# Two neighbourhood attentions of a two-block model: where the attention steps of the third and fourth head group stand among the weight products

## The chip, the core and the metric

The kernel runs on one core of a Trainium2 chip. Its engines are TensorE (PE), VectorE (DVE), ScalarE (ACT), GpSimd (POOL) and SyncE (SP); each works through its own instructions in order, and they meet through semaphores. The metric is the device time in microseconds of one execution, the median over several.

## The reference

Two blocks run one after the other on x of 256 tokens by 1024 features, in float32. The first has a dilated attention, an mLSTM and two SwiGLU feed-forwards. The second has four layers, each a mixer and an MLP with squared ReLU; the mixers are neighbourhood attention (layer 0), a conformer convolution (1), a short gated convolution (2) and neighbourhood attention again (3). Beside the 256 latent tokens the second block has 256 context tokens; they are carried along up to layer 2, so layer 0 computes attention for both, layer 3 for the latent tokens alone. This is the attention, cut:

```python
def neighbourhood_attention(h_lat, h_ctx, wqkv, wo, rpb, ctx_out):
    q, k, v = split_heads(h_lat @ wqkv, 3)          # 16 heads of 64
    q = q * ATTN_SCALE
    if ctx_out:
        q_c, k_c, v_c = split_heads(h_ctx @ wqkv, 3)
    else:
        k_c, v_c = split_heads(h_ctx @ wqkv[:, D_MODEL:], 2)
...
        s_lat = jnp.einsum("bhqd,bhaqkd->bhqak", q_r, k_nb)   # window of the latent grid
        s_lat = s_lat + bias_r                                 # a bias by relative position
        s_ctx = jnp.einsum("bhqd,bhcd->bhqc", q_r, k_c)
        p = jax.nn.softmax(jnp.concatenate([s_lat, s_ctx], axis=-1))
        return p_lat @ v_nb + p_ctx @ v_c
...
    o_lat = o_grid @ wo
    if ctx_out:                                     # context tokens attend to context only
        p_c = jax.nn.softmax((q_c * ATTN_SCALE) @ k_c.T)
        o_ctx = (p_c @ v_c) @ wo
    return o_lat, o_ctx
```

## The kernel before

Activations lie feature-major: 8 tiles of 128 features, each 256 latent and 256 context columns wide. Every weight is read once as a **unit** of up to 1024 rows by 256 columns (1 MB). SP loads it into one of three `raw` buffers; ACT rounds it to `hi` and DVE takes the rest, `lo = raw - hi` (a **split**, two halves of 128 x 1024 on each engine, L1359, L1360, L1656, L1659). A product is three fp32r matmuls (hi x hi, hi x lo, lo x hi; L1149 to L1151 feature-major, L1170 to L1172 for token-major values). There are two buffers of split halves and three raw ones, so the split of a unit waits until the unit two before it is used, and the load of a unit until the split of the unit three before it is done.

`plan()` writes the program as one list of steps; each engine goes through this list and issues its part of each step. So the order of the list is the order on every engine. The split of unit j + 1 is written just ahead of the products of unit j. `linear` and `linear_tok` write the products of a unit; between them they call `advance`, which takes the next step of the first entry of `background`. `adv` says how many steps are taken in one tile of a unit (8 contraction steps k), spread evenly by `share`; `outer=True` runs both tiles of a unit together, k by k. A bare `yield True` in a background generator is a step that writes nothing.

`neighbourhood` takes the 16 heads in four groups of four heads (`group`), two heads to a tile `q` of 128 features. For each group it writes three units: q, k and v. Behind them the group's attention `heads(group)` goes into `background`, and is so spread over the three units of the next group. The attention of a group has these steps:

- `lat_scores(q, qb)`, four in a group: the scores of one block `qb` of 128 latent queries for two heads, into two PSUM banks (PE, L1282); DVE adds the bias table and takes the maximum (L1938), negates it (L1947), ACT takes the exponentials (L1547), DVE the reciprocal (L1949) and scales (L1953). DVE's part stands in one piece in its order, so it holds DVE while ACT works. It also writes `table(i + 2)`.
- `ctx_scores(q)`, two in a group and in layer 0 only: the context queries (PE L1291; DVE L1961, L1964, L1968; ACT L1558).
- `turn(n, q, which)`: transposes of the probabilities through the identity (PE L1302), copied back by ACT (bank one, L1565) and DVE (bank two, L1973).
- `mix(q, ctx, ...)`: probabilities by values (PE L1314); ACT rounds the result to the high half of `OB` (L1570), DVE makes the low half (L1978).

The bias tables (`table(i)`, i from 0 to 15, one for each latent score step) are POOL's: four DMAs from `na_rpb` into `NB` (L2119), a wait for them, two additions of the mask (L2123). There are two table buffers, so table i + 2 waits until DVE has taken the maximum of score step i (L1947 reads it).

After the last group `grow` writes the four units of the output projection `na_wo_2`. Its first unit runs both tiles together; before its contraction step k the function from `stages_for` takes steps from the background until the tile k of the attention's output is made, and then `adv` 6 asks for more. Since `heads(3)` enters the background just ahead of it, all attention of the last group lies in this first unit. PSUM banks are handed out in turn, six of them, so the bank numbers change when steps change places. `credit` and `pace` decide at the end of tiles whether a row of the modulation matrix is computed on DVE (L1735), with its DMA on POOL.

## Time and profile before

| | us |
|---|---|
| median of 3 runs | 3013.59 |
| lowest, highest | 3011.38, 3013.71 |
| the profiled execution, its device time | 3015.04 |
| its span, first to last instruction | 3013.1 |
| PE busy in it | 2899.0 (96%) |
| DVE busy | 2000.8 (66%) |
| ACT busy | 1197.6 (40%) |
| POOL busy | 352.4 (12%) |

The span is cut by the place in the program. Layer 0's attention runs from about 869 to 1140 us, layer 3's from about 2600 to 2815. A matmul's duration in the trace contains its way through the array, so matmuls that follow each other overlap; what one costs PE is the distance between two starts. A wait is shown in brackets behind the row that ended it, with the instruction that it waited for. The granted clock (PEclk) is the share of TensorE's full 2.4 GHz, 0.5 being the lower level of 1.2 GHz. In the rows "NB" stands for the bias tables too, since they lie in the same memory, and "PB", "PT" for the probabilities and their transposes.

### The profile page before, as it was taken

To read this page: it belongs to the slowest core of one execution; us is meant where nothing else is said; L and a number is where in the kernel's file an instruction comes from. 1 tells how busy PE (TensorE), PEld (TensorE's weight loads), DVE (VectorE), ACT (ScalarE), POOL (GpSimd) and SP (SyncE) were. 2 spreads that over 40 slices of the span, in tenths; PEclk is the share of its full clock that TensorE was granted. 3 is DMA by queue.
4 is the path that set the end of the run, shared out by engine and by line. 5 is a ranking of instruction groups with operands and counts; after the bars stand their busy time and mean duration, and the time that the engine had idled before them with its cause. 6 is when DMAs were issued, how large, how long until landed. Compare 5 with 4: busy or idle time off the path is not lost.

```text
span 3013.1 us, 42743 instructions
## 1 busy us (share of the span) xinstructions
PE 2899.0 (96%) x17730; PEld 2511.1 (83%) x17730; DVE 2000.8 (66%) x3252; ACT 1197.6 (40%) x1953; POOL 352.4 (12%) x545
## 2 busy tenths in 40 slices
PE   7999999989999989999999999999999999998998
PEld 7999998879977768888864888888888888876998
DVE  6776777658745557777644776777777667654665
ACT  5444444644444434223312632223234222443543
POOL 0000000000113220000122100001010000243000
PEclk9999999989999999999999999999999999999999
DMA  6444675347755523544464254553535545565453
GB/s 216 154 154 140 212 239 190 127 140 246 238 113 84 83 56 123 171 155 159 129 188 119 84 161 161 161 168 122 166 125 168 161 154 169 125 107 82 136 186 127
DMA packets 362275, 451.88 MB, mean 150 GB/s; under 512 B 12656, under 2 KB 332432, under 8 KB 362080
## 3 DMA queue, kind: packets, MB, share of 16 engines
q1 hardware_dynamic: 326976, 329.89, 33.7%
q0 software_dynamic: 34944, 118.65, 16.5%
q8 instruction: 140, 2.29, 0.3%
q10 hardware_dynamic: 160, 0.59, 0.1%
q14 instruction: 55, 0.45, 0.0%
HBM read 438.67 MB, written 1.05 MB: 146 GB/s over the span
## 4 chain that ended last, share of the span: by engine, by line
PE 84%; DVE 9%; ACT 4%; DMA 1%; issue 1%; POOL 1%; DVEq 0%; ACTq 0%; POOLq 0%
PE ps L1149 24%; PE ps L1151 24%; PE ps L1150 24%; PE ps L1327 2%; PE ps L1170 2%; PE ps L1171 1%; PE ps L1172 1%; DVE lo L1656 1%; PE ps L1314 1%; DVE NB L1690 1%; DVE lo L1659 1%; ACT hi L1359 1%; PE ps L1302 1%; PE ps L1282 1%; PE ps L1182 1%
## 5 line engine op out<-in xcount | busy, mean ns | idle before, releaser
L1149 PE MATMUL ps<-XN,hi 128*128 128x256 f32 (+1 forms) x3120 | 1037.3, 332 | 46.0 <-DVE XN L1903 11.3
L1150 PE MATMUL ps<-XN,hi 128*128 128x256 f32 (+1 forms) x3120 | 1020.1, 327 | 0.0
L1151 PE MATMUL ps<-XN,lo 128*128 128x256 f32 (+1 forms) x3120 | 1019.6, 327 | 0.0
L1149 PEld LDWEIGHTS ps<-XN,hi 128*128 128x128 f32 x3120 | 598.7, 192 | 122.4 <-issue 14.5
L1151 PEld LDWEIGHTS ps<-XN,lo 128*128 128x128 f32 x3120 | 598.9, 192 | 49.0
L1150 PEld LDWEIGHTS ps<-XN,hi 128*128 128x128 f32 x3120 | 599.4, 192 | 47.6
L1735 DVE CUSTOM_DVE_ANT_0 MX<-MW,C 128x1024 bf16<-128x1024 f32 x384 | 480.0, 1250 | 109.3 <-DMA MW<-in_mod_w 102.5
L1656 DVE TENSOR_TENSOR lo<-raw,hi 128x1024 fp32r<-128x1024 f32 (+1 forms) x313 | 383.9, 1227 | 242.7 <-ACT hi L1359 241.6
L1359 ACT ACTIVATE hi<-raw 128x1024 fp32r<-128x1024 f32 (+1 forms) x313 | 326.2, 1042 | 428.6 <-PE ps L1151 428.4
L1659 DVE TENSOR_TENSOR lo<-raw,hi 128x1024 fp32r<-128x1024 f32 (+1 forms) x313 | 380.3, 1215 | 0.0
L1149 PE MATMUL ps<-H,hi 128*128 128x512 f32 (+1 forms) x1072 | 380.2, 355 | 0.0
L1150 PE MATMUL ps<-H,hi 128*128 128x512 f32 (+1 forms) x1072 | 379.7, 354 | 0.0
L1151 PE MATMUL ps<-H,lo 128*128 128x512 f32 (+1 forms) x1072 | 379.7, 354 | 0.0
L1360 ACT ACTIVATE hi<-raw 128x1024 fp32r<-128x1024 f32 (+1 forms) x313 | 324.6, 1037 | 0.0
L2078 POOL DMA_DIRECT2D MW<-in_mod_w x192 | 103.0, 537 | 1451.0 <-DVE mod L1735 1341.6
L1150 PEld LDWEIGHTS ps<-H,hi 128*128 128x128 f32 x1072 | 202.7, 189 | 28.4
L1149 PEld LDWEIGHTS ps<-H,hi 128*128 128x128 f32 x1072 | 202.7, 189 | 28.2
L1151 PEld LDWEIGHTS ps<-H,lo 128*128 128x128 f32 x1072 | 202.7, 189 | 28.0
L1727 DVE SCALAR_TENSOR_TENSOR X<-ps,mod,X 128x256 f32<-128x256 f32 x244 | 108.2, 479 | 139.1 <-PE ps L1151 139.1
L2084 POOL TENSOR_TENSOR SA<-SA,NB 128x256 f32<-128x256 f32 (+1 forms) x69 | 70.4, 1020 | 812.5 <-ACT NB L1367 811.7
L1170 PE MATMUL ps<-hi,XN 128*128 128x256 f32 x512 | 151.5, 296 | 0.1
L1171 PE MATMUL ps<-lo,XN 128*128 128x256 f32 x512 | 145.5, 284 | 0.0
(239 smaller groups left out, 3402.8 us busy)
## 6 DMA issues: line engine op xcount, KB each, us to landing
raw<-in_mlp_w SPq DMA_DIRECT2D x128, 1024.0 KB, 5.4
MW<-in_mod_w POOLq DMA_DIRECT2D x192, 512.0 KB, 3.8
raw<-in_ffn_w_in SPq DMA_DIRECT2D x44, 1024.0 KB, 5.1
raw<-in_attn_w_in SPq DMA_DIRECT2D x36, 1024.0 KB, 4.8
raw<-in_na_wqkv SPq DMA_DIRECT2D x24, 1024.0 KB, 5.4
raw<-in_ffn_w_out SPq DMA_DIRECT2D x16, 1024.0 KB, 5.3
raw<-in_mlstm_w_in SPq DMA_DIRECT2D x12, 1024.0 KB, 5.0
raw<-in_cv_w SPq DMA_DIRECT2D x12, 1024.0 KB, 6.2
```

The lines of the kernel that those rows point to most:

```text
L1149: e.matmul(out, whi, xhi, start=first, stop=False)
L1150: e.matmul(out, whi, xlo, start=False, stop=False)
L1151: i = e.matmul(out, wlo, xhi, start=False, stop=last)
L1170: e.matmul(out, xhi, hi[:, k, :], start=k == 0, stop=False)
L1171: e.matmul(out, xhi, lo[:, k, :], start=False, stop=False)
L1359: e.activation(hi[:, a:b], raw[:, a:b], ACT.Copy).then_inc(*high.says(("hi", j, 0)))
L1360: e.activation(hi[:, b:c], raw[:, b:c], ACT.Copy).then_inc(*high.says(("hi", j, 1)))
L1656: e.tensor_tensor(lo[:, a:b], raw[:, a:b], hi[:, a:b].bitcast(F32), ALU.subtract).then_inc(*low.says(("lo", j, 0)))
L1659: e.tensor_tensor(lo[:, b:c], raw[:, b:c], hi[:, b:c].bitcast(F32), ALU.subtract).then_inc(*low.says(("lo", j, 1), ("spent", j)))
L1727: e.scalar_tensor_tensor(out=m.X[:, j, a:b], in0=src[:, a:b], scalar=mod_of(m, gate, j, i), in1=m.X[:, j, a:b], op0=ALU.mult, op1=ALU.add) ...
L1735: e.tensor_tensor_reduce(out=m.MX[:, :], in0=m.MW[:, :], in1=m.C[:, s, :], scale=1.0, scalar=0.0, op0=ALU.mult, op1=ALU.add, accum_out=m.m ...
L2078: e.dma_start(m.MW[:, :], T["mod_w_2"][n // 48][n % 48 * P:(n % 48 + 1) * P, :]).then_inc(*sig["mw"].says(("mod_raw", n)))
```

## The change

All of it is in `neighbourhood`, so both layers 0 and 3 are touched.

- In `heads`: an empty step after the first two scores; the score step of the second query tile's second block comes ahead of the first tile's mix in layer 3 (it stood behind it); in layer 0 an empty step more ahead of that mix; ahead of every mix a loop yields until the group's values are made.
- In the loop over groups: for group 3 `heads(3)` enters the background behind the units of q and k, ahead of v. In group 3's units `adv` rises: q from 2 to 4 and k from 2 to 4 in layer 0, q from 1 to 2 and k from 2 to 3 in layer 3. The value unit has `adv` 3 in place of 2 in layer 0, for all groups, and in layer 3 for group 3. These units carry the third group's attention (`heads(2)`), group 3's value unit also the start of `heads(3)`.
- For groups 0 to 2 the background is drained before the next group's attention enters it. Two loops that did part of this are gone.

```diff
--- before.py
+++ after.py
@@ -803,6 +803,7 @@
         yield True
         s1 = lat_scores(0, 1)
         yield True
+        yield True
         for q in range(2):
             turn(s0, q, 0)
             yield True
@@ -815,12 +816,19 @@
             if q == 0:
                 s0 = lat_scores(1, 0)
                 yield True
+            if q == 0 and not ctx_out:
+                s1 = lat_scores(1, 1)
+                yield True
+            if ctx_out:
+                yield True
+            while ("v", layer, group) not in p.made:
+                yield True
             mix(q, False, *lat)
             yield True
             if ctx_out:
                 turn(sc, q, 2)
                 yield True
-            if q == 0:
+            if ctx_out and q == 0:
                 s1 = lat_scores(1, 1)
                 yield True
             if ctx_out:
@@ -829,8 +837,6 @@
 
     for group in range(4):
         def evac_q(t, b, u):
-            while len(p.background) > 1:
-                p.advance()
             p.do("na_q", layer, group, t, n, b, u)
 
         def evac_k(t, b, u):
@@ -840,15 +846,21 @@
             p.do("na_v", layer, group, t, b, u)
 
         streams = group == 0 and not ctx_out
-        p.linear("na_wqkv_2", slot, 0, KT, group * 256, 256, ("xn", s, 0, n), evac_q, adv=2 if ctx_out else 1,
-                 outer=group == 0, streams=(0,) if streams else None)
-        p.linear("na_wqkv_2", slot, 0, KT, 1024 + group * 256, 256, ("xn", s, 0, 512), evac_k, adv=2,
-                 outer=streams, streams=(0, 1) if streams else None)
-        p.linear_tok("na_wqkv_2", slot, 2048 + group * 256, 256, 4, ("xn", s, 0, 512), evac_v, adv=2)
+        p.linear("na_wqkv_2", slot, 0, KT, group * 256, 256, ("xn", s, 0, n), evac_q,
+                 adv=4 if ctx_out and group == 3 else 2 if ctx_out or group == 3 else 1, outer=group == 0,
+                 streams=(0,) if streams else None)
+        p.linear("na_wqkv_2", slot, 0, KT, 1024 + group * 256, 256, ("xn", s, 0, 512), evac_k,
+                 adv=4 if ctx_out and group == 3 else 3 if group == 3 else 2, outer=streams, streams=(0, 1) if streams else None)
         p.flush()
-        while len(p.background) > 1:
-            p.advance()
-        p.background.append(heads(group))
+        if group == 3:
+            p.background.append(heads(group))
+        p.linear_tok("na_wqkv_2", slot, 2048 + group * 256, 256, 4, ("xn", s, 0, 512), evac_v,
+                     adv=3 if ctx_out or group == 3 else 2)
+        p.made.add(("v", layer, group))
+        p.flush()
+        if group < 3:
+            p.drain()
+            p.background.append(heads(group))
     p.grow(("ob", layer, 0, n), n, (layer, 2), "na_wo_2", slot,
            p.stages_for(lambda k: ("ob", layer, k) in p.made), 6)
```

The order of the instructions shows it at two places. The first is PE in layer 0, around the first scores of the last group (`KB,QB` are scores, `OB` products of the output projection, `XN` with 256 columns products of the value unit; the digit after `ps` is the PSUM bank). Before:

```order
L1151 MATMUL ps3<-OB,lo1 128x512
L1282 MATMUL ps5<-KB,QB 128x512
L1282 MATMUL ps0<-KB,QB 128x512
L1149 MATMUL ps2<-OB,hi1 128x512
L1150 MATMUL ps2<-OB,hi1 128x512
L1151 MATMUL ps2<-OB,lo1 128x512
L1149 MATMUL ps3<-OB,hi1 128x512
L1150 MATMUL ps3<-OB,hi1 128x512
L1151 MATMUL ps3<-OB,lo1 128x512
L1282 MATMUL ps1<-KB,QB 128x512
L1282 MATMUL ps4<-KB,QB 128x512
```

With the change (its line numbers are 12 higher):

```order
L1184 MATMUL ps2<-hi0,XN 128x256
L1294 MATMUL ps3<-KB,QB 128x512
L1294 MATMUL ps4<-KB,QB 128x512
L1182 MATMUL ps2<-hi0,XN 128x256
L1183 MATMUL ps2<-lo0,XN 128x256
L1184 MATMUL ps2<-hi0,XN 128x256
L1182 MATMUL ps2<-hi0,XN 128x256
L1183 MATMUL ps2<-lo0,XN 128x256
L1184 MATMUL ps2<-hi0,XN 128x256
L1294 MATMUL ps5<-KB,QB 128x512
L1294 MATMUL ps0<-KB,QB 128x512
```

The last group's first two scores stood between products of `na_wo_2`; now they stand between products of the value unit, one unit earlier.

The second is DVE at the end of layer 3's attention, from the last latent softmax to the first residual (`lo<-raw,hi` is a weights' split, `OB` a mix's low half, `PT` a copy of a transpose, `X` the residual). Before:

```order
L1938 ISA stat 128x1
L1947 TENSOR_SCALAR stat<-stat 128x2
L1949 RECIPROCAL stat<-stat 128x2
L1953 TENSOR_SCALAR PB<-PB,stat 128x512 x2
L1973 COPY PT<-ps 128x4x128 x2
L1978 TENSOR_TENSOR OB<-ps,OB 128x256
L1727 SCALAR_TENSOR_TENSOR X<-ps,mod,X 128x256 x2
```

With the change:

```order
L1959 TENSOR_SCALAR stat<-stat 128x2
L1961 RECIPROCAL stat<-stat 128x2
L1965 TENSOR_SCALAR PB<-PB,stat 128x512 x2
L1668 TENSOR_TENSOR lo<-raw,hi 128x1024
L1671 TENSOR_TENSOR lo<-raw,hi 128x1024
L1990 TENSOR_TENSOR OB<-ps,OB 128x256
L1985 COPY PT<-ps 128x4x128 x2
L1990 TENSOR_TENSOR OB<-ps,OB 128x256
L1739 SCALAR_TENSOR_TENSOR X<-ps,mod,X 128x256 x2
```

A split now stands between the last softmax and the copies of the last transposes, and with it the low half of the other mix.

## Rows read from the trace of the kernel before

**Rows 1.** The page, busy time, share and count of PE and its loads.

```profile
PE 2899.0 (96%) x17730; PEld 2511.1 (83%) x17730; DVE 2000.8 (66%) x3252; ACT 1197.6 (40%) x1953; POOL 352.4 (12%) x545
```

**Rows 2.** Windows: stretch, its us, then PE, PEld, DVE, ACT, POOL, PEclk, DMA.

```profile
1000.20:1053.90 53.70, 52.74 (x321) 40.06 (x320) 28.84 (x64) 23.52 (x57) 16.13 (x25) 1.00 0.55 89
1053.90:1102.50 48.60, 37.21 (x187) 23.23 (x186) 25.19 (x62) 17.16 (x46) 7.83 (x12) 0.93 0.23 33
2761.10:2796.10 35.00, 23.89 (x130) 16.93 (x129) 15.92 (x41) 11.16 (x25) 8.51 (x14) 0.80 0.30 46
2704.80:2708.80 4.00, 3.99 (x20) 3.88 (x20) 1.24 (x2) 0.60 (x1) 0.00 (x0) 0.57 0.81 134
```

**Rows 3.** PE's timeline, layer 0, squeezed unit: start, us, instruction, [idle before <-releaser].

```profile
1083.51 0.57 PE L1149 MATMUL ps<-OB,hi 128*128 128x512 f32 x1 [2.98 <-DVE OB L1978]
...
1093.58 3.27 PE L1314 MATMUL ps<-PT,VB 128*64 128x256 f32 x16 [3.86 <-DVE PT L1973]
```

**Rows 4.** PE's timeline, layer 0, ahead of the squeezed unit and at its start.

```profile
1049.74 1.95 PE L1314 MATMUL ps<-PT,VB 128*64 128x256 f32 x16 [0.96 <-DVE PT L1973]
...
1052.08 0.28 PE L1170 MATMUL ps<-hi,XN 128*128 128x256 f32 x1
1052.20 0.28 PE L1171 MATMUL ps<-lo,XN 128*128 128x256 f32 x1
...
1054.72 0.40 PE L1149 MATMUL ps<-OB,hi 128*128 128x512 f32 x1
1054.95 0.39 PE L1150 MATMUL ps<-OB,hi 128*128 128x512 f32 x1
```

**Rows 5.** DVE's timeline, layer 0: two latent score steps, a context one.

```profile
1059.38 0.69 DVE L1938 CUSTOM_DVE_ANT_0 PB<-ps,NB 128x512 f32<-128x512 f32 x1 [1.25 <-PE ps L1282]
...
1063.60 0.67 DVE L1938 CUSTOM_DVE_ANT_0 PB<-ps,NB 128x512 f32<-128x512 f32 x1
...
1068.29 1.28 DVE L1961 TENSOR_REDUCE stat<-ps 128x2 f32<-128x512 f32 x2
...
1072.35 0.68 DVE L1973 COPY PT<-ps 128x512 f32<-128x512 f32 x1
```

**Rows 6.** Groups of DVE instructions, 1000 to 1104: count, busy, mean ns, idle before.

```profile
L1973 DVE COPY PT<-ps 128x512 f32<-128x512 f32 x13 | 8.9, 686 | 6.9 <-PE ps L1302 6.9
...
L1659 DVE TENSOR_TENSOR lo<-raw,hi 128x1024 fp32r<-128x1024 f32 x4 | 4.9, 1216 | 0.0
...
L1978 DVE TENSOR_TENSOR OB<-ps,OB 128x256 fp32r<-128x256 f32 x9 | 3.8, 420 | 9.7 <-ACT OB L1570 9.7
```

**Rows 7.** POOL's timeline, layer 3: issues of bias tables and one table's additions.

```profile
2677.96 2.44 POOL L2119 DMA_DIRECT2D NB<-in_na_rpb  x4 [0.92 <-DVE stat L1947]
...
2722.62 2.44 POOL L2119 DMA_DIRECT2D NB<-in_na_rpb  x4 [0.92 <-DVE stat L1947]
2729.85 3.00 POOL L2123 TENSOR_TENSOR NB<-NB,cst 128x256 f32<-128x256 f32 x2 [4.79 <-DMA NB<-in_na_rpb]
...
2742.84 2.44 POOL L2119 DMA_DIRECT2D NB<-in_na_rpb  x4
...
2753.75 2.45 POOL L2119 DMA_DIRECT2D NB<-in_na_rpb  x4
...
2766.56 2.43 POOL L2119 DMA_DIRECT2D NB<-in_na_rpb  x4 [4.58 <-DVE stat L1947]
...
2774.98 2.44 POOL L2119 DMA_DIRECT2D NB<-in_na_rpb  x4
```

**Rows 8.** PE's timeline, layer 3: second group's transposes; last product step of the squeezed unit.

```profile
2704.81 1.50 PE L1302 MATMUL ps<-cst,PB 128*128 128x128 f32 x7 [2.00 <-DVE PB L1953]
...
2795.26 0.39 PE L1149 MATMUL ps<-OB,hi 128*128 128x256 f32 x1 [0.95 <-DVE OB L1978]
```

**Rows 9.** DVE's timeline, layer 3: a split's second half; the last bias table's use.

```profile
2730.48 1.76 DVE L1659 TENSOR_TENSOR lo<-raw,hi 128x1024 fp32r<-128x1024 f32 x1
...
2783.51 0.69 DVE L1938 CUSTOM_DVE_ANT_0 PB<-ps,NB 128x512 f32<-128x512 f32 x1 [1.05 <-POOL NB L2123]
```

## Prediction

> **What bounds the kernel now.** The page first: TensorE (PE) is busy for 96% of the span [rows 1], so time can only be won where PE waits or runs at the lower of its two clock levels. Then PE's timeline over both attentions. One place stands out in each: the first unit of the output projection (`na_wo_2`, columns 0 to 255), into which the whole attention of the last group is squeezed (scores, softmax, transposes, mixes), since its steps begin only there. In the first attention (layer 0, with context) that unit lasts 48.6 us at a granted clock of 0.93, in the second (layer 3) 35.0 us at 0.80 [rows 2]. PE waits there for VectorE (DVE), most of all for 2.98 and 3.86 us in layer 0 [rows 3], 0.95 us at the end of layer 3 [rows 8], with shorter waits between.
>
> How much is lost? Count PE's own work. Matmuls back to back follow each other in 0.23 us where 512 columns pass and in 0.12 us where 256 do (1054.72 to 1054.95, 1052.08 to 1052.20 [rows 4]). In layer 0 I count from the first unit beside the third group's steps (S = 1000.2) to the end of the squeezed unit (1102.5). Products: 48 matmuls each for q, k and `na_wo_2` at 0.23 (33.1) and 96 for v at 0.12 (11.5), 44.6 us. What a group's attention costs PE follows from the stretch 1000.2 to 1053.9 [rows 2], which holds q, k and v (33.6) and exactly one group's worth of steps: 53.7 - 33.6 - 0.96 of wait (1049.74 [rows 4]) = 19.1 us. Two groups, and one mix of 1.0 left over from the group before: 44.6 + 38.2 + 1.0 = 83.8. It took 102.3 us, so **18.5 us are lost** to waits and slow clock.
>
> Layer 3, 2716.6 to 2796.1, took 79.5 us: products 34 (192 matmuls at 0.12, 48 at 0.23), two groups without context about 25 (19.1 scaled by 10 steps of 16, mixes counted alike), so 20 are lost.
>
> **The change, part by part.** Nothing is computed more or less. All engines issue the same instructions, GpSimd (POOL) in the same order, PE, DVE and ScalarE (ACT) in another.
>
> *The last group's attention begins behind its keys; the third group's steps lie about twice as dense, to be through by then.* What must be paid is DVE's serial time, since each softmax holds DVE while ACT takes the exponentials. A latent score step holds it for 4.22 us (1059.38 to 1063.60), a context one for 4.06 (1068.29 to 1072.35) [rows 5]; a split of weights costs 2.4, a copy of a transpose 0.69, the low half of a mix 0.42 [rows 6]. From S on: 8 x 4.22 + 4 x 4.06 + 4 x 2.4 + 12 x 0.69 + 8 x 0.42 = 71.3, with one row of modulations (taken like a split, 2.4) 73.7 us. PE's own work from S is now 82.8 (the left-over mix goes ahead of S and nets nothing). So in layer 0 PE can stay the bound, if each result comes in time. I walked both engines through the new order with these durations. The waits I find, from S: 1.0 before the first transposes of group 2; 0.4 before the second transposes of group 3; 2.0 for a bank whose mix is finished only behind the weights' split, half of it given back at the next wait; 0.8 before the last latent mix, 0.8 before the last context mix, 0.9 for its halves before the last product. It ends 88.3 after S: 5.5 are lost in place of 18.5, a gain of 13. I keep 12, since a wait of 2 us can bring slow clock: behind the wait of 2.00 at 2704.81 [rows 8] the granted clock is 0.57 over 4 us [rows 2], near 1.2 GHz, where full clock would save 1.7. **Layer 0: -12.**
>
> *Layer 3 has another queue in it: the bias tables.* Each latent score needs a table that POOL makes: 4 DMAs, a wait for them, two additions. Table i+2 is issued once score i's maximum is taken, and POOL makes one after another, in 10.9 us (2742.84 to 2753.75) or, with no weights coming in, 8.4 (2766.56 to 2774.98) [rows 7]. From table 6 to the last POOL idles only three times: 0.92, 0.92 and 4.58 us, each for a score's maximum (2677.96, 2722.62, 2766.56 [rows 7]). The new order can take away these gaps, no more. The last table is there at 2783.5 now, and DVE waits for it (1.05 [rows 9]); it will be there at 2783.5 - 6.4 = 2777.1. Behind it stand its softmax (4.2), then a weights' split, which the change puts between this softmax and what follows (2.4), the low half of a mix and two copies (1.8), the last mix (1.95 [rows 4], up to 3.4 at half clock), and five of the eight steps of products in place of one (30 matmuls at 0.12 are 3.6 us, 6.4 at half clock): 2791 to 2795. The old end is 2796.1 (2795.26 [rows 8] and six matmuls). PE waits on the way, as I walk it, 1.2, 1.8, 5.2 (the second transposes of the last group, whose score waits for table 13), 2.9 and 1.7 us; they take the place of the old ones. **Layer 3: -3.**
>
> *The extra step between scores and transposes, the drains between groups.* In groups 0 and 1 the first transposes come four products later. They don't wait before, so this buys nothing. In layer 3 the second query tile's two scores now stand next to each other, ahead of the mix, but with a weights' split still between them on DVE: the wait of 2.00 at 2704.81 [rows 8] becomes about 1.5. That is inside the -3. In layer 0 the value unit gets crowded (DVE some 17 us of work in 23 of PE), and a wait near 1 us before the latent mix, as at 1049.74 [rows 4], stays: 0.
>
> *The wait added.* The loop that holds a mix until its group's values are made turns for the last group alone; what it delays PE would wait for anyway. The drains empty the queue of steps between groups, which is empty or one mix long there: 0. Of the late split in layer 3 one thing more hangs: the load of the unit three further on, which SyncE issues behind it. Three units of PE work cover that: 0. If that cover were gone, PE would wait for a whole load, some 5 us.
>
> Sum: 3015.0 (the profiled run; its span is 3013.1) - 12 - 3 = 3000.0. That run is 1.4 above the median, so the median moves from 3013.6 to **2998.5**.
>
> **Where a rule speaks against it.** Beside a DVE split POOL's two additions take 3.00 us (2729.85 [rows 7]), and the split's second half takes 1.76 (2730.48 [rows 9]) where its mean is 1.22 [rows 6]. The Trainium skill, "SBUF — State Buffer", section "Who interferes with whom", states the rule: a DVE instruction with both inputs in SBUF and a GpSimd instruction that reads it take turns for a shared port. The rows agree with it, and a denser DVE meets it more often; what that would do to the tables is priced in rival 2 from the rows.
>
> **The rivals.**
> 1. *The tables land faster.* If all six from table 10 on take 8.4 us, the last lands at 2720.8 (table 9's end, 2721.7, less the first gap) + 50.4 = 2771.2 and the unit ends 6 earlier than above: layer 3 -9, time 2992.5. Against it: the same weights' loads run in the same stretch. 12%.
> 2. *The tables are stretched, or the dense third group costs PE more.* Four tables at 12 us (10.9, and the additions 1 us longer, as at 2729.85) put the last at 2785.6 and the end at about 2801, layer 3 +5: 3006.5. Or DVE, which stands still behind each softmax, makes PE wait 7 us more in layer 0: 3005.5. Together 16%.
> 3. *Slower than before: the table queue outgrows the gain.* At 13 us for each of the six the last lands at 2798.8, layer 3 +18. In layer 0 the last two tables can start only with the last group's first maxima, at about 1050, and at 13 each its gain shrinks from 12 to 2: 3029. It decides from 12 us a table on, where the gain is gone. For it: the queue has no slack in layer 3. Against it: 10.9 is the longest the rows show from table 10 on. 4%.
>
> That the change doesn't bite (the scores stand earlier for PE, but wait for DVE's turn) is bounded by DVE's 73.7 us against PE's 82.8; what it can cost is in rival 2.
>
> **How the numbers follow.** 0.2% (6 us) is about what a measurement of this kernel can tell from no change. Forecast (2994 to 3003) 66%, rival 1 12%, rival 2 16% (a third of it within 0.2%), rival 3 4%, something unseen 2%. Faster 0.88, same 0.07, slower 0.05. The range takes in rival 1 and most of rival 2: 2990 to 3007.
>
> **What would show it.** Right: the squeezed unit of layer 0 ends some 12 us earlier, with no wait over 2 us from S on; in layer 3 POOL has no gap from table 6 to the last, DVE waits for POOL before three or four scores, PE waits some 5 us before the last group's second transposes, and on DVE a split lies between the last softmax and the last copies. Wrong: tables no longer back to back; waits of over 5 us in sum in the last group's value unit of layer 0; or a stretch outside the two attentions that changes its length.

## The result: 0.18% slower, not 0.5% faster

The changed kernel takes 3020.1 us (median of 13 runs, 3016.9 to 3021.8) beside 3013.7 us for the kernel before in the same series (13 runs). The ratio is 1.0018, interval 1.0011 to 1.0026. The forecast was 2998.5. The profiled execution has a span of 3019.7 us where the one before has 3013.1.

Page of the kernel after, busy time, share and count by engine:

```profile
PE 2905.5 (96%) x17730; PEld 2514.7 (83%) x17730; DVE 2001.6 (66%) x3252; ACT 1197.8 (40%) x1953; POOL 352.1 (12%) x545
```

DVE, ACT and POOL do the same work as before. PE is "busy" 6.5 us longer than in [rows 1] with the same matmuls, and the span is 6.6 us longer. So in sum PE idles as long as before and works more slowly; its idle time has only moved.

**Where it is lost.** Two landmarks enclose each attention on DVE: the last residual row ahead of it, and the first residual behind its output projection. First before, then after (start, duration, instruction, [idle <-releaser]):

```profile
842.65 3.25 DVE L1928 SCALAR_TENSOR_TENSOR X<-X,PV,RS 128x256 f32<-128x256 f32 x8 [2.64 <-ACT RS L1374]
...
1102.07 1.66 DVE L1727 SCALAR_TENSOR_TENSOR X<-ps,mod,X 128x256 f32<-128x256 f32 x4 [1.05 <-PE ps L1151]
...
2597.46 0.48 DVE L1706 SCALAR_TENSOR_TENSOR X<-ps,mod,X 128x256 f32<-128x256 f32 x1
...
2795.92 0.88 DVE L1727 SCALAR_TENSOR_TENSOR X<-ps,mod,X 128x256 f32<-128x256 f32 x2 [0.72 <-PE ps L1151]
```

```profile
843.15 3.26 DVE L1940 SCALAR_TENSOR_TENSOR X<-X,PV,RS 128x256 f32<-128x256 f32 x8 [2.64 <-ACT RS L1386]
...
1105.82 1.66 DVE L1739 SCALAR_TENSOR_TENSOR X<-ps,mod,X 128x256 f32<-128x256 f32 x4 [1.05 <-PE ps L1163]
...
2602.89 0.47 DVE L1718 SCALAR_TENSOR_TENSOR X<-ps,mod,X 128x256 f32<-128x256 f32 x1
...
2802.36 0.88 DVE L1739 SCALAR_TENSOR_TENSOR X<-ps,mod,X 128x256 f32<-128x256 f32 x2 [2.59 <-PE ps L1163]
```

**Stretch A** (layer 0) grew from 259.4 to 262.7 us, **stretch B** (layer 3) from 198.5 to 199.5, and what lies between them from 1495.4 to 1497.1. A and B are read below from every kernel in the same way. Kernels with the same layer 0 give A within 0.4 us (259.0 to 259.4 for the layer 0 of before) or 0.9 us (262.7 and, in l0only below, 263.6 for the changed one), so a difference of 1 us in A says little. B is a looser measure; see the first experiment. Ahead of A the program is the same in all kernels, and still its length lies anywhere from 842.6 to 845.8 us in their traces.

**Layer 0.** The stretches of [rows 2] again, the second one 3.4 us longer, since it ends later:

```profile
1000.20:1053.90 53.70, 47.74 (x248) 33.24 (x247) 29.47 (x66) 22.11 (x52) 16.08 (x25) 0.94 0.47 69
1053.90:1105.90 52.00, 45.29 (x269) 31.99 (x268) 25.19 (x62) 18.68 (x50) 7.86 (x12) 0.93 0.28 51
```

The second row still holds the end of the value unit: the first product of `na_wo_2` starts at 1072.82, where it started at 1053.94. The squeezed unit did get shorter, some 33 us in place of 48.6. But the stretch ahead of it, where PE was busy for 52.74 of 53.70 us at full clock, now has 6 us idle and a granted clock of 0.94. PE waits there and a little later for something that the kernel before never waits for, copies by ACT out of PSUM (four of the six largest waits of PE in stretch A: us, times, longest; the other two belong to the norm and stand in both kernels):

```profile
PE ps L1326 <- DVE PT L1985: 4.9, 5, 1.9
PE ps L1161 <- ACT VB L1550: 3.5, 1, 3.5
PE ps L1314 <- ACT QB L1539: 2.8, 1, 2.8
PE ps L1326 <- ACT KB L1545: 2.3, 1, 2.3
```

The three waits on PE's timeline, with what ACT did just before; an excerpt of the timelines of PE and ACT after:

```profile
1013.08 0.72 ACT L1559 ACTIVATE PB<-PB,stat 128x512 f32<-128x512 f32 x1 [2.70 <-DVE stat L1959]
...
1014.50 0.57 ACT L1539 ACTIVATE QB<-ps 128x512 f32<-128x512 f32 x1
...
1015.13 0.98 PE L1314 MATMUL ps<-cst,PB 128*128 128x128 f32 x4 [2.79 <-ACT QB L1539]
...
1037.53 0.57 ACT L1545 ACTIVATE KB<-ps 128x512 f32<-128x512 f32 x1
...
1038.24 1.08 PE L1326 MATMUL ps<-PT,VB 128*64 128x256 f32 x8 [2.26 <-ACT KB L1545]
...
1076.79 0.36 ACT L1550 ACTIVATE VB<-ps 128x256 f32<-128x256 f32 x1
...
1077.20 0.80 PE L1161 MATMUL ps<-OB,hi 128*128 128x512 f32 x1 [3.53 <-ACT VB L1550]
```

Read the first trio. ACT sat idle for 2.70 us ahead of an exponential (L1559), because DVE had not yet given the negated maximum. Behind the exponentials in ACT's order stands the copy of a finished q tile (L1539), though the last product of that tile had begun at 1010.39 and the copy begins at 1014.50. PE's next transposes want the very PSUM bank that this copy empties. So a score's lateness on DVE passes through ACT's queue and a bank to PE, which had nothing to do with that score. Ahead of the other two copies ACT's exponentials waited for DVE in the same way, 3.95 and 3.08 us. After each of the three the clock is low:

```profile
1015.20:1018.60 3.40, 3.40 (x10) 2.37 (x10) 1.20 (x3) 0.36 (x1) 2.07 (x4) 0.52 0.07 25
...
1038.30:1042.00 3.70, 3.70 (x15) 2.54 (x16) 0.86 (x3) 0.38 (x1) 3.34 (x6) 0.62 0.65 89
...
1077.20:1083.80 6.60, 6.60 (x23) 3.73 (x24) 4.30 (x5) 2.23 (x3) 1.32 (x2) 0.52 0.22 58
```

These are windows of the kernel after (stretch, us, PE, PEld, DVE, ACT, POOL, PEclk, DMA). 0.52 is near the level of 1.2 GHz; at full clock the work of these 13.7 us would take 3.4 x 0.52 + 3.7 x 0.62 + 6.6 x 0.52 = 7.5, so 6.2 are lost. With the waits' 8.6 that is 14.8 us, near the 15.3 that separate +3.3 from the forecast -12. That the two sums are near each other is in part luck: when the experiment below removes the banks' part, A gives back 9.8.

The sharing of the bank can be read from the order alone. Rows of the order of the kernel after on PE at the first two places (the digit behind `ps` is the bank):

```
L1163 MATMUL ps3<-XN,lo0 128x512
L1314 MATMUL ps2<-cst,PB2 128x128 x4
L1314 MATMUL ps3<-cst,PB2 128x128 x4
...
L1163 MATMUL ps0<-XN,lo1 128x512
L1326 MATMUL ps0<-PT2,VB 64x256 x4
```

A tile of products ends in bank 3, and four matmuls later the transposes want bank 3; a mix wants bank 0 right behind a k tile. Banks are handed out in turn, and a tile's bank is taken at its beginning, so it is the "oldest" at its end although it is the last to be emptied. The kernel before has one such place in layer 0 (a mix a few steps behind a v tile); PE does not wait there. In stretch B of the kernel after PE waits 6.8 us in sum for copies of k and v tiles, in the kernel before not at all.

**Layer 3.** Tables 10 to 12 and the last one, timeline of POOL after; then what waits for them and what stands behind, from the timelines of PE and DVE:

```profile
2728.44 2.44 POOL L2131 DMA_DIRECT2D NB<-in_na_rpb  x4 [3.73 <-DVE stat L1959]
...
2738.10 2.43 POOL L2131 DMA_DIRECT2D NB<-in_na_rpb  x4
2748.87 1.43 POOL L2135 TENSOR_TENSOR NB<-NB,cst 128x256 f32<-128x256 f32 x2 [8.34 <-DMA NB<-in_na_rpb]
2750.24 2.44 POOL L2131 DMA_DIRECT2D NB<-in_na_rpb  x4
2757.07 3.33 POOL L2135 TENSOR_TENSOR NB<-NB,cst 128x256 f32<-128x256 f32 x2 [4.40 <-DMA NB<-in_na_rpb]
...
2785.48 1.42 POOL L2135 TENSOR_TENSOR NB<-NB,cst 128x256 f32<-128x256 f32 x2 [4.66 <-DMA NB<-in_na_rpb]
```

```profile
2774.32 1.97 PE L1314 MATMUL ps<-cst,PB 128*128 128x128 f32 x8 [6.11 <-DVE PB L1965]
...
2786.93 0.69 DVE L1950 CUSTOM_DVE_ANT_0 PB<-ps,NB 128x512 f32<-128x512 f32 x1 [2.43 <-POOL NB L2135]
...
2792.32 1.23 DVE L1668 TENSOR_TENSOR lo<-raw,hi 128x1024 fp32r<-128x1024 f32 x1 [1.21 <-ACT hi L1371]
```

Much of the picture is the one forecast: a wait of 6.11 us before the last group's second transposes (5.2 forecast), three waits of DVE for a table (12.9 us in sum, 1.1 before), a split between the last softmax and the last copies. But POOL is not back to back, it still waits 3.73 us for a maximum, and the last table is ready at 2786.9. Less the 5.4 us that layer 3 starts later, this is 2781.5: 2 us earlier than before, not 6.4.

### The profile page after: what moved, and what is told of

Its sections match the earlier page's. It is cut to its first block, busy times and chain, and to the rows that moved or that the text cites. A ratio compares the mean times of both kernels' runs of the same rounds, so it can differ in the third digit from the quotient of the medians.

```text
span 3019.7 us, 42736 instructions
## 1 busy us (share of the span) xinstructions
PE 2905.5 (96%) x17730; PEld 2514.7 (83%) x17730; DVE 2001.6 (66%) x3252; ACT 1197.8 (40%) x1953; POOL 352.1 (12%) x545
## 4 chain that ended last, share of the span: by engine, by line
PE 83%; DVE 8%; ACT 4%; DMA 2%; issue 1%; POOL 1%; DVEq 0%; ACTq 0%; POOLq 0%
PE ps L1161 24%; PE ps L1163 24%; PE ps L1162 24%; PE ps L1339 2%; PE ps L1182 2%; PE ps L1183 1%; PE ps L1184 1%; DVE lo L1668 1%; PE ps L1326 1%; DVE lo L1671 1%; PE ps L1314 1%; DVE NB L1702 1%; DMA NB<-in_na_rpb 1%; ACT hi L1371 1%; PE ps L1294 1%
```

## The experiments

Each kernel ran beside the kernel before. Kernel and ratio with its interval, then stretches A and B of the profiled execution, in us:

| kernel | median us | ratio to before | A | B |
|---|---|---|---|---|
| before | 3013.0 to 3016.5 | 1 | 259.4 | 198.5 |
| after | 3020.1 | 1.0018 (1.0011 to 1.0026) | 262.7 | 199.5 |
| l0only | 3016.5 | 1.0001 (0.9992 to 1.0010) | 263.6 | 194.2 |
| l3only | 3017.6 | 1.0004 (0.9995 to 1.0014) | 259.0 | 200.3 |
| lru_before | 3014.8 | 0.9995 (0.9986 to 1.0004) | 258.0 | 198.4 |
| lru_after | 3006.9 | 0.9969 (0.9957 to 0.9980) | 252.9 | 196.6 |
| dense_lru | 3023.1 | 1.0026 (1.0014 to 1.0037) | 262.9 | 200.1 |
| even_lru | 3004.6 | 0.9966 (0.9953 to 0.9979) | 249.5 | 196.3 |
| even_turn | 3026.1 | 1.0044 (1.0027 to 1.0060) | 267.0 | 199.5 |
| late_even | 3004.6 | 0.9969 (0.9957 to 0.9981) | 248.4 | 196.5 |
| notab3_before | 3010.3 | 0.9984 (0.9975 to 0.9994) | 259.4 | 192.1 |
| notab3_lru | 2992.6 | 0.9924 (0.9909 to 0.9939) | 253.0 | 179.8 |
| pipe_before | 3014.2 | 1.0008 (0.9998 to 1.0017) | 259.0 | 195.3 |
| pipe_after | 3018.6 | 1.0019 (1.0010 to 1.0028) | 263.3 | 199.2 |
| pipe_even | 3006.7 | 0.9976 (0.9966 to 0.9985) | 249.9 | 196.0 |
| ahead_even | 3011.6 | 0.9992 (0.9983 to 1.0002) | 255.3 | 193.8 |
| ahead_after | 3027.2 | 1.0046 (1.0031 to 1.0061) | 266.6 | 202.3 |
| best | 3005.2 | 0.9970 (0.9958 to 0.9982) | 249.6 | 195.5 |

The median of the kernel before itself moved between 3013.0 and 3016.5 from one series to the next, so a ratio is the thing to compare, not two medians.

### One layer at a time

Both versions of `neighbourhood` stand in one kernel; layer 3 calls the old one in l0only, layer 0 in l3only:

```diff
-    neighbourhood(p, 3, 1, False)
+    neighbourhood_old(p, 3, 1, False)
```

> Layer 0 with the change, layer 3 as before. The offset of the residual rows between the two traces grew by 3.8 us over layer 0's attention, by 1.5 in the conformer and by 1.0 over layer 3's. If the loss is made in layer 0 (theory), this kernel is 3.5 to 5.5 us slower than the kernel before. If the table queue of layer 3 makes it (rival), it is within 2 us of it.

> Layer 3 with the change, layer 0 as before. Theory: 0 to 2 us slower than before, since the last table is ready 3.4 us later in the trace after and the drain of the order gives part of it back. Rival (layer 3's tables are the cause): 4 us or more slower.

Neither ratio leaves 1 by more than its interval, so the totals do not place the loss; by the time alone l0only would speak for the rival. The traces do place it for layer 0: A is 263.6 in l0only, 259.0 in l3only. For layer 3 they showed something unasked for: B is 194.2 in l0only, where layer 3's instructions are those of the kernel before, against 198.5; that hides the 4.2 us of A in the total. In l0only POOL takes 12.6 and 9.9 us from the issue of tables 8 and 9 to the next issue, in before 13.2 and 11.0, which is 1.7 of the 4.3 us. It looks as if a layer that hangs on a queue of DMAs answers to where it starts relative to other loads; the size is 4 us here, the cause was not tested. A difference of 1 us in B alone proves nothing. Held against l0only, whose layer 0 is the same, the changed layer 3 costs 5.3 us (199.5 to 194.2); held against before, 1.0.

### Banks by age

The oldest bank is no longer the one handed out longest ago but the one given back longest ago; a tile gives its bank back at its end. It is so in the two attentions alone. The diff to the kernel after, cut:

```diff
+        if self.oldest:
+            b = min((b for b in range(NBANK) if b not in self.open), key=lambda b: self.stamp[b])
+            self.released(b)
...
             self.open.difference_update(b for b, _ in banks)
+            self.released(*[b for b, _ in banks])
```

> The changed kernel, but in both attentions a PSUM bank is chosen by when its last user gave it back (the oldest first), not in turn, so that no step takes a bank that an ACT copy of q, k or v has just begun to empty. Theory (banks held by ACT's copies, which stand behind exponentials): the waits of PE for QB, KB and VB (2.8, 2.3 and 3.5 us in layer 0, 6.8 in sum in layer 3) go, and the slow clock behind them; layer 0 6 to 9 us shorter than after, layer 3 0 to 3, so 3010 to 3014 us where the kernel after has 3020. Rival (DVE's serial time in the dense third group, or the tables): 3018 to 3021, the waits come back under DVE's names.

> The kernel before with the same choice of banks. Theory: its trace has no wait for QB, KB or VB in layer 0, so nothing is to be had, within 3 us of the kernel before. If the choice of banks is worth something of itself, whatever the order, it is 5 us faster or more.

lru_after is at 0.9969, and A falls from 262.7 to 252.9. Of these 9.8 us 5.1 are idle time of PE (20.7 to 15.6) and 4.7 its busy time (242.0 to 237.3), that is, clock. The expected 3010 to 3014 was too little. Waits of PE in its stretch A:

```profile
PE ps L1344 <- DVE PT L2003: 5.3, 5, 1.9
PE ps L1344 <- ACT VB L1568: 2.8, 1, 2.8
```

QB and KB are gone. VB is there still, but at L1344, a mix: it waits for the values themselves, no longer for their bank. And the transposes that waited 2.79 us for ACT's copy run straight on; lru_after, the first transposes of the third group:

```profile
1013.31 1.09 PE L1332 MATMUL ps<-cst,PB 128*128 128x128 f32 x8 [0.91 <-DVE PB L1983]
```

The same edit does nothing for the kernel before (0.9995), as expected: the banks are a fault that the new order meets, not one that was there. The rival (DVE's serial time, or the tables) is out for layer 0: neither was touched, and 0.5% of the whole time came back. In layer 3 it is half right. B falls by 2.9 us, but what PE no longer waits for banks it waits for DVE and for the values: PB 8.7 to 11.9 us, and VB at a mix 4.3.

### The denser third group alone

In lru_before, only the `adv` of group 3's q and k:

```diff
-evac_q, adv=2 if ctx_out else 1,
+evac_q, adv=(4 if ctx_out else 2) if group == 3 else 2 if ctx_out else 1,
-evac_k, adv=2,
+evac_k, adv=(4 if ctx_out else 3) if group == 3 else 2,
```

> The order of the kernel before with the banks chosen by age, and of the change only the denser third group (steps per tile of group 3's q and k units: 4 and 4 in layer 0, 2 and 3 in layer 3); the last group's attention still begins with the output projection. The same kernel without the denser group took 3014.8 us. Theory: the density alone costs little, 0 to 3 us (3015 to 3018), and gains nothing. Rival (DVE is too slow for the dense group): 3020 or more.

The rival is right: 1.0026 against 0.9995, some 9 us, of which A shows 4.9 and B 1.7; 2.6 more lie ahead of A in the two traces, where nothing differs, so the density itself is worth less than 9. The place is telling, two rows of PE in its squeezed unit:

```profile
1068.82 1.46 PE L1321 MATMUL ps<-cst,PB 128*128 128x128 f32 x8 [3.04 <-DVE PB L1972]
...
1089.52 0.51 PE L1168 MATMUL ps<-OB,hi 128*128 128x512 f32 x1 [3.70 <-DVE OB L1997]
```

Three of the four tiles of the value unit behind the dense stretch have no attention step beside them now, so DVE stands idle there (9.45 us ahead of 1062.19), and the last group's chain still begins only at the squeezed unit. Density is an outlay; only the early start of the last group pays it back. Together, with the banks right, they are worth lru_after against lru_before, 0.9969 to 0.9995: 8 us.

### The crowded value unit of the first groups

```diff
-adv=4 if ctx_out and group == 3 else 2 if ctx_out or group == 3 else 1,
+adv=(4 if group == 3 else 3) if ctx_out else 2 if group == 3 else 1,
...
-adv=4 if ctx_out and group == 3 else 3 if group == 3 else 2,
+adv=(4 if group == 3 else 3) if ctx_out else 3 if group == 3 else 2,
...
-adv=3 if ctx_out or group == 3 else 2)
+adv=3 if group == 3 else 2)
```

> The changed kernel with banks by age (3006.9 us), but in layer 0 the steps of groups 0 and 1 lie evenly in the next group's units (q, k, v with 3, 3, 2 steps a tile; the changed kernel has 2, 2, 3), and in layer 3 the value units of groups 1 and 2 are as before. The trace of lru_after has a wait of 1.85 us at 995.65 before the second group's last latent mix, and slow clock behind it (0.97 over 940 to 1000). Theory: this is the crowded value unit, it goes, 2 to 4 us faster (3003 to 3005). Rival: the wait only moves: within 1 us of 3006.9.

> even_lru (3004.6 us) with the banks handed out in turn again. The order of its steps still has three places in layer 0 where a step takes a bank that an ACT copy has just begun to empty (transposes behind q's first tile, a mix behind k's, the second product row behind v's), the same three as the changed kernel. Theory (banks): 8 to 13 us slower than even_lru, 3012 to 3018. Rival (the even spread is what helped): 3004 to 3009.

even_lru: A is 249.5, 3.3 less than in lru_after, and 9.9 less than before. The ratios (0.9966 and 0.9969) do not tell the two apart; the stretch does, since the wait of 1.85 us and the slow clock behind it are gone (1.00 over 940 to 1000). even_turn is the sharpest test of the banks: the same order of steps as even_lru, another hand-out. It is 0.8% slower, more than expected, because two of its other groups meet the fault too. Three rows of its waits in stretch A:

```profile
PE ps L1314 <- ACT QB L1539: 8.5, 5, 2.8
...
PE ps L1161 <- ACT VB L1550: 3.6, 1, 3.6
...
PE ps L1326 <- ACT KB L1545: 2.3, 1, 2.3
```

They sum to 14.4 us, and A differs by 17.4. Alone, without the banks, the even spread would look like a failure: 1.0044 beside the 1.0018 of the kernel after.

### The wait for the last values

```diff
             if q == 0:
+                while ("v", layer, group) not in p.made:
+                    yield True
                 s0 = lat_scores(1, 0)
```

> even_lru (3004.6 us), but the last group's third score step comes behind its last value tile, so that ACT copies the values before these exponentials. The waits for VB before the first mix (2.96 us in layer 0, 5.5 in layer 3) go. Theory (DVE's serial chain is the bound there, and the wait only shows it): what goes comes back at the next waits, and the later score costs 0 to 4 us: 3004 to 3009. Rival (the wait is a loss of its own): 3 us faster or more.

Equal to even_lru (0.9969 and 0.9966; A 1.1 shorter, B 0.2 longer). Theory holds: both waits for VB are gone and the time is the same. In layer 0 the last latent mix now waits 2.45 us where it waited 1.04, so half of the 2.96 comes back at once; the 1.1 us in A are hardly more than its spread.

### The tables of layer 3

notab3_before and notab3_lru leave out tables 2 to 15 of layer 3 (`if i + 2 < 16 and layer == 0`; the score steps read table 0 or 1).

> The kernel before, but in layer 3 only the first two bias tables are made and used for all sixteen score steps: fourteen tables (DMAs and additions of POOL) are left out, and no score step waits for one. Theory (the table queue bounds layer 3 only at its end, where DVE waits 1.05 us for the last one): 1 to 4 us faster than the kernel before. Rival (the queue is what makes layer 3 20 us longer than PE's work): 8 us faster or more.

> The changed kernel with banks by age, and in layer 3 the same fourteen tables left out. In its trace DVE and PE wait for tables before the last scores (PE 5.8 us at most for PB). Theory: with the change the queue of tables is what holds the last group, so without it layer 3 is 8 to 12 us shorter: 2995 to 2999 us. Rival (DVE's own serial time holds it): within 3 us of 3006.9.

Both theories have the right mechanism and too small a size. Without the queue B falls by 6.4 in the old order (the ratio gives 1.8 to 7.5 us; and 4.3 of such a difference can arise with unchanged instructions, as in l0only) and by 16.8 in the new one (196.6 to 179.8), where 8 to 12 were expected. The last 31 us ahead of the first residual of layer 3, first even_lru (tables), then notab3_lru:

```profile
2754.40:2785.40 31.00, 23.24 (x150) 18.54 (x151) 12.09 (x27) 9.72 (x23) 5.41 (x9) 0.83 0.35 49
```

```profile
2743.50:2774.60 31.10, 27.26 (x200) 21.63 (x200) 15.74 (x41) 12.20 (x28) 0.00 (x0) 1.00 0.21 67
```

In the kernel before POOL's wait for a table's DMAs is 4.1 to 9.4 us in layer 3 behind four issues of 0.61 us; each moves 64 KB and lands 4.1 us after its issue at the least, 5.0 in the median. By the Trainium skill, "DMA: Bandwidth & Descriptors", section "Anatomy of one DMA — SWDGE (gpsimd) path", a DMA of 64 KB would take about 2.15 us, an estimate from its fit; no row here is as low as that, and the rows decide.

So in layer 3 the new order (with the banks by age) is worth 12.3 us of B without the tables (192.1 in notab3_before to 179.8) and 1.8 with them (198.4 in lru_before to 196.6). These kernels leave out POOL's additions and the DMAs together; which of the two holds the layer they do not say. Two attempts to get at the rest. The first splits a table's step and puts the additions of table i + 1 ahead of the DMAs of table i + 2:

```diff
-            if i + 2 < 16:
-                table(i + 2)
+            if i + 1 < 16:
+                added(i + 1)
+            if i + 2 < 16:
+                table(i + 2)
```

> even_lru (3004.6 us) with the bias tables in two stages: at score step i POOL first adds the mask to table i + 1, whose DMAs were issued a step earlier, and then issues the DMAs of table i + 2. The wait for the DMAs (4.3 to 9.4 us in each table of before) so lies beside the next step and holds nothing. Theory: most of the 13.6 us that the tables cost the changed kernel in layer 3 come back, 8 to 13 us: 2992 to 2997. Rival: the DMAs themselves are the limit, and two in flight slow each other: 3001 to 3005.

> The changed kernel itself (banks in turn) with the tables in two stages. Theory: layer 0 keeps its loss of 3.3 us, layer 3 gets shorter by 8 us or more: 3008 to 3012 us, beside 3020 for the changed kernel. Rival (banks in layer 3 are as bad as the tables): 3015 to 3019.

> The kernel before with the tables in two stages. Leaving fourteen tables out of layer 3 gave 3.6 to 4.8 us there. Theory: 2 to 5 us faster than before, no more, since the old order is bound by DVE's serial work at its end. Rival: as pipe_even, 8 us or more.

All three missed: even_lru and pipe_even are alike in B (196.3, 196.0), so are after and pipe_after (199.5, 199.2). B of pipe_before is 3.2 shorter than in before at 1.0008 of the time, less than the 4.3 that l0only shows for the same instructions. POOL of pipe_even shows why, and it was readable beforehand:

```profile
2741.64 2.44 POOL L2155 DMA_DIRECT2D NB<-in_na_rpb  x4
2751.89 1.40 POOL L2162 TENSOR_TENSOR NB<-NB,cst 128x256 f32<-128x256 f32 x2 [7.80 <-DMA NB<-in_na_rpb]
```

POOL is an engine in order, and its list runs ahead of the score steps: right behind the issue of table i + 2 stand that table's own additions, of the next step, and their wait. Nothing was taken apart. The second attempt has the issue ahead of the other table's additions, so that two tables are on their way:

```diff
+            if i + 2 < 16:
+                table(i + 2)
             if i + 1 < 16:
                 added(i + 1)
-            if i + 2 < 16:
-                table(i + 2)
```

> even_lru (3004.6 us) with the DMAs of table i + 2 issued ahead of the additions of table i + 1, so that two tables are on their way at once. Theory (POOL's serial chain issue, wait, additions costs the changed kernel 13.6 us in layer 3): 6 to 13 us faster than even_lru, 2992 to 2999, and POOL's waits for NB shrink from 4.3 to 9.4 us to under 3. Rival (the DMAs' own throughput is the limit, or waiting for the maximum of step i before the additions costs as much): 3003 to 3008.

> The changed kernel itself (banks in turn) with the same edit. Theory: layer 3 is 5 to 12 us shorter than in the changed kernel, 3008 to 3014. Rival: 3018 to 3022.

Also missed in time, though the mechanism bit. From the third table of layer 3 on POOL of ahead_even waits for DMAs only once, 2.88 us at the last table; now it waits for DVE:

```profile
2758.06 2.44 POOL L2155 DMA_DIRECT2D NB<-in_na_rpb  x4 [8.31 <-DVE stat L1983]
2760.51 1.41 POOL L2162 TENSOR_TENSOR NB<-NB,cst 128x256 f32<-128x256 f32 x2
2763.74 2.58 POOL L2155 DMA_DIRECT2D NB<-in_na_rpb  x4 [1.82 <-DVE stat L1983]
```

A new ring has closed: the maximum of score i releases the issue of table i + 2, behind that stand the additions of table i + 1, behind these the maximum of score i + 1. The shortest turn takes 5.7 us (2758.06 to 2763.74), where DVE needs 4.2 for a score [rows 5]. In layer 3, where a table had taken 8.4 to 13 us in even_lru, that gains 2.4 us (B 193.8 against 196.3); in layer 0, where tables were no limit, it loses 5.8 (A 255.3 against 249.5). In the changed kernel it gains nothing even in B (202.3 against 199.5): PE waits 8.1 us for the copies of v tiles there in place of 5.6. Why these come later was not followed up. The last kernel does it in layer 3 alone.

> even_lru (3004.6 us) with the DMAs of table i + 2 ahead of the additions of table i + 1 in layer 3 alone. From the stretch between the last residual before an attention and the first behind it: layer 0 as in even_lru (249.5 us), layer 3 as in ahead_even (193.8, where even_lru has 196.3). Theory: the two layers add up, 3001 to 3004 us. Rival (ahead_even's layer 3 owes its gain to another phase of the weights' loads): 3004 to 3008.

The layers did not add up: B is 195.5, not 193.8, and 0.9970 is even_lru's 0.9966 within the intervals. Only 0.7 of the 2.4 us is left when layer 0 goes back, which fits the rival (another phase of the loads) and does not prove it. How to free the 16.8 us that the tables still hold in lru_after, with a third table buffer or with fewer and earlier DMAs, was not tried and stays open.


## Why the prediction was wrong

**Layer 0, -12: the walk left out an engine.** "I walked both engines through the new order" is the step that failed. The walk had PE and DVE in it, and took PSUM banks as free when the step that used them was done. The third engine, ACT, empties the banks of q, k and v in its own order, behind exponentials that wait for DVE. The missing terms are three waits of 2.8, 2.3 and 3.5 us and the slow clock behind each, held at nothing in the prediction; removing their cause gave back 9.8 us of A. With the banks by age the waits are near those of the walk:

| wait of PE | predicted | in even_lru |
|---|---|---|
| first transposes, third group | 1.0 | 0.2 (0.9 in lru_after) |
| second transposes, last group | 0.4 | none |
| a bank behind the split | 2.0 | none; 3.0 for the last values in its place |
| last latent mix | 0.8 | 1.04 |
| last context mix | 0.8 | 0.88 |
| last product | 0.9 | 0.93 |

With the banks alone (lru_after) A is 6.5 us shorter than before, about half of the forecast 12; it takes the even spread, another order than the predicted one, to make it 9.9. The wait of 2.96 us for the last values, with a granted clock of 0.57 over the 4 us behind it, is on no list of the prediction. (The waits it lists add up to 4.9 us, not to its 5.5; that changes nothing here.) The prediction did allow that a wait for a bank could come; it looked for it at a mix, not at a copy behind exponentials.

**Extra steps and drains, 0.** Mis-sized. "A wait near 1 us before the latent mix stays" was said of the value unit; the denser value unit of groups 0 and 1 made it 1.91 us in the kernel after, with a granted clock of 0.60 behind it, where the kernel before waits 0.95 and keeps its clock (1.00 from 995.86 on). Spreading it again gave 3.3 us of A (lru_after to even_lru).

**The dense third group.** It was held at nothing, with 7 us in rival 2. Alone it costs 4.9 us of A (dense_lru against lru_before). Rival 2's mechanism was not the one that decided, though: the banks cost A twice as much. Whether the early start covers the cost of the density in full no run shows; no kernel has the early start without it.

**Layer 3, -3.** It was +1.0 (B, a measure with 4 us of play), or -1.9 with better banks. Two sizes failed in the table queue. The gap ahead of table 10 was to vanish; it is 3.73 us (2728.44), because the score whose maximum it waits for stands behind a split (both halves, 2724.22 to 2726.9 on DVE). And a table was held at 10.9 us at most, though an earlier one in the trace of before takes 13.2 (2698.39 to 2711.58); from the issue of table 11 to that of table 12 it took 12.1 (2738.10 to 2750.24), the next one 10.1 with additions of 3.33 beside a split. So the last table came 4.4 us later than worked out (2781.5 in before's time, not 2777.1), and the end followed it as forecast, 15.4 us behind (2786.93 to 2802.36). That the tables are the bound there notab3_lru shows; their weight, 16.8 us, is far more than the prediction made of it.

**The rest of the program, 0.** Between the two attentions it grew by 1.7 us (1495.4 to 1497.1), which the prediction named as a sign of being wrong. The values of this stretch do not scatter evenly. It is 1495.0 to 1495.5 in the five kernels that keep the old place of the last group in both layers, 1496.2 to 1497.7 in the twelve with a changed layer 0, and 1496.5 in l3only, where all up to its end is as before. In the traces of after, lru_after and l3only 1.0 to 1.5 us of it arise at one place, at the end of the conformer, some 600 us behind the first residual. PE waits 1.53 or 1.54 us there in all kernels; the 5 us behind that wait, before and after (stretch, us, PE, PEld, DVE, ACT, POOL, PEclk, DMA):

```profile
1703.06:1708.06 5.00, 4.97 (x36) 4.51 (x37) 1.46 (x5) 2.50 (x6) 0.21 (x1) 1.00 0.56 187
```

```profile
1706.97:1711.97 5.00, 4.97 (x23) 4.51 (x24) 0.23 (x1) 1.59 (x4) 0.00 (x0) 0.66 0.56 188
```

The same instructions with the same wait in front go at full clock in one kernel and near the lower level in the other. So a change can cost time in a part that it does not touch, and l3only has the same loss without any change ahead of it. What decides it no run shows, and it is not the whole of the difference: two of the twelve (ahead_after, pipe_even) have full clock there and are still at 1496.3 or more.

**The range.** For layer 3 rival 2 came nearest: it put the last table 8.5 us later than the forecast and the layer at +5; it was 4.4 and +1.0. No rival had the right cause in layer 0. A case "the loss lies in the banks" was not among the rivals, though the order of the instructions shows the bank numbers.

## What to carry to other kernels

When steps are moved among matmuls, redo the walk for every engine that empties PSUM, not for the one that computes, and look in the order for a step that takes a bank just behind the step that filled it: a copy that is short (0.57 us) can stand behind exponentials that wait for a third engine. Hand out buffers by when they come free, not by when they were taken, before judging an order; the same order of steps was 0.8% apart between the two (even_lru and even_turn). And when a change packs the consumers of a slow queue closer together, first take the queue out to see what the packing is worth.

The Trainium skill, "Perfetto Trace Analysis", section "Optimization Strategy", says that a repeated gap on the engine that should be saturated can mean too little PSUM or SBUF for the next tile. Here there were three such gaps in layer 0, behind QB, KB and VB, and the number of banks was not the fault: six banks sufficed once they were handed out by age.

## What the runs showed of the hardware

A layer bound by a queue of small DMAs can change its length with the kernel around it: the same instructions of layer 3 took 198.5 us in one kernel and 194.2 in another. That it is the phase against the large loads is argued, not shown. And PE's granted clock fell behind each of the three waits of 2.3 to 3.5 us in layer 0, to 0.52 or 0.62, and took 6.2 us more where the waits took 8.6. The waits near 1 us at the end of even_lru's squeezed unit had full clock around them:

```profile
1084.50:1093.40 8.90, 7.09 (x45) 5.13 (x46) 2.13 (x5) 1.36 (x3) 0.00 (x0) 1.00 0.00 0
```

So here waits of 2.3 to 3.5 us cost nearly twice their length, waits of 1 us only their own. Between them the length alone does not decide: behind a wait of 1.64 us (before, at 940.65) the clock was 1.00 over 4 us, behind 1.91 (after, at 994.07) 0.60, and behind the same wait of 1.53 to 1.54 us in the conformer 1.00 in seven kernels and 0.66 to 0.68 in the other eleven.
